# Output projection of a two-layer decoder step: weights in 4 + 4 row tiles, split while values are summed; the first quarter in two passes of tokens; GpSimd reads four page numbers ahead

## The chip, the cores and the metric

The kernel runs on one core of one Trainium2 chip. The metric is the device time of one execution in microseconds (us), as the median of several runs. Engines: TensorE (PE; its weight loads are listed apart as PEld), VectorE (DVE), ScalarE (ACT), GpSimd (POOL) and SyncE (SP), which issues DMAs. Each engine has its own instruction queue, and the queues meet only at semaphores.

## What is computed

One inference step of a trunk of two layers, for 256 prompt tokens and 8 x 8 = 64 sample tokens, 320 token columns in all, with 1024 features. Cut to the part around the change:

```python
for l in range(DEPTH):                      # 2 layers
    x = x + 0.5 * swiglu(rmsnorm(x), ...)   # ffn 1
    h = rmsnorm(x)
    # past: pages of keys and values of 8 sample sequences, 8 pages of 128 positions each
    oa = moba_attend(...)                   # heads 0..5
    of = fox_attend(...)                    # heads 6..10
    oc = hgrn2_recurrence(...)              # heads 11..15
    x = x + concat(oa, of, oc) @ w_out[l]   # (tokens x 1024) @ (1024 x 1024)
    x = x + 0.5 * swiglu(rmsnorm(x), ...)   # ffn 2
y = rmsnorm(x)
```

## The kernel before

Everything is written by hand in one block per engine, in program order, with counted semaphores. Features lie on the 128 partitions, tokens in the free dimension. A float32 product is made of three matmuls in a rounded type (`fp32r`): for each weight tile `whi` x `xh`, `wlo` x `xh` and `whi` x `xl`, where `hi` is the value rounded by an ACT copy, and `lo` is what DVE gets by subtracting `hi` from the value.

Weights go through two slots, 0 and 1. SP loads `raw[s]`, ACT rounds it to `whi[s]` (helper `hi`, line 609 before), DVE makes `wlo[s]` (helper `lo`, line 894), and PE multiplies (helper `dense`, line 1505). SP may load `raw[s]` again when `wlo[s]` is made (`split_done[s]`), and ACT may write `whi[s]` again when PE has used both (`w_free[s]`, which the order of instructions below prints as `weights_free`). The semaphore `raw_in[s]` tells that `raw[s]` has landed, `wout_in` that the extra pieces of the output weights have.

Attention over the past works in 32 blocks of two pages for each layer, four blocks a query (one query is one of the 8 sample sequences, `q`). PE turns the keys (line 1664) and makes scores (1688). For the query before, it turns the weights (`turn_weights`, 1699 and 1703), sums the values over 8 pages (`values`, 1715 and 1717, then the new ones, 1721 and 1723) and turns the outputs (`turn_outputs`, 1731). DVE copies weights (`copy_weights`, 1182 and 1185), scales the outputs (`scale_outputs`, 1194) and copies them (`copy_outputs`, 1203 to 1206). The prompt's attention and the recurrence are done among these blocks and are ready before the last query. Value pages are loaded by GpSimd (`load_values`, lines 582 and 583): for each page it waits until the query before has used that page (`values_used`), reads the page number from a table (`value_load`) and issues two DMAs. Value pages of query 7 are loaded after PE has used those of query 6, in two halves of four pages.

Behind query 7 comes the output projection, in four quarters `p` of 256 output features. A quarter has 8 tiles of 128 input rows: five in slot 0 and three in slot 1. The input is `mixed`, rounded to `oh` by ACT (prompt tokens at line 829, sample tokens at 869), and DVE makes `ol` (prompt 1408 in `prompt_out_lo`, sample 1471). Input tile 5 is made of rows 640 to 703 and 960 to 1023, and so has a DMA of its own for each half. Each quarter has two output tiles `j` in two PSUM banks; when one is complete (`acc_ready`, or `w_free[1]` for the second), DVE adds it to the residual `X` and makes the squares and the next `xl` (`accumulate`: lines 916, 908, 909, 903), and ACT makes the next `xh` (623). Over all 320 tokens a quarter is 8 x 2 x 3 = 48 matmuls. DVE's order in a quarter is `lo(1, u)`, `lo(0, u + 1)`, `accumulate`, where `u` is the quarter's use of the slots and `u + 1` the next one, so slot 0 is split a quarter ahead. After the last quarter come the gate weights of ffn 2, eight tiles in each slot.

## Time and profile before

| | |
|---|---|
| median of 3 runs | 1786.49 us (1783.93 to 1787.73) |
| profiled execution | 1789.04 us, of which its span, first to last instruction, is 1787.4 us |
| mean granted clock of TensorE over the span | 0.959 of full speed |
| busy: PE, DVE, ACT, POOL | 1663.8, 1084.8, 669.8, 162.1 us |
| instructions | 36002 |

All times in the rows below are from the start of the span of the profiled execution. A row of a timeline has an instruction's start, its duration, and in brackets how long its engine was idle before it and what ended that. Matmuls are pipelined, so the difference of two starts, not the duration, is what one costs in a stream. A granted clock of 1.00 is 2.4 GHz and one of 0.50 is 1.2 GHz.

### The profile page before, as it was taken

To read this page: it belongs to the slowest core of one execution; us is meant where nothing else is said; L and a number is where in the kernel's file an instruction comes from. 1 tells how busy PE (TensorE), PEld (TensorE's weight loads), DVE (VectorE), ACT (ScalarE), POOL (GpSimd) and SP (SyncE) were. 2 spreads that over 40 slices of the span, in tenths; PEclk is the share of its full clock that TensorE was granted. 3 is DMA by queue.
4 is the path that set the end of the run, shared out by engine and by line. 5 is a ranking of instruction groups with operands and counts; after the bars stand their busy time and mean duration, and the time that the engine had idled before them with its cause. 6 is when DMAs were issued, how large, how long until landed. Compare 5 with 4: busy or idle time off the path is not lost. (4 is left out here: it accounts for less than half of the span.)

```text
span 1787.4 us, 36002 instructions
## 1 busy us (share of the span) xinstructions
PE 1663.8 (93%) x13569; PEld 1537.6 (86%) x13569; DVE 1084.8 (61%) x1815; ACT 669.8 (37%) x960; POOL 162.1 (9%) x329
## 2 busy tenths in 40 slices
PE   5999999979989789999999999999798887999997
PEld 5999999966667579999999999999566666999996
DVE  7666555456577556665566665543676755766645
ACT  3333232235544424333333323322565443433332
POOL 0000000021333300000000000000224331000000
PEclk9999999989989889999999999999899997999998
DMA  6444445546666634444444444554657574444443
GB/s 191 141 154 152 139 145 141 156 135 185 216 195 214 195 125 160 146 143 151 140 154 155 150 135 153 159 141 126 188 182 243 191 217 147 160 159 141 138 151 116
DMA packets 284179, 287.46 MB, mean 161 GB/s; under 512 B 26542, under 2 KB 272998, under 8 KB 283942
## 3 DMA queue, kind: packets, MB, share of 16 engines
q1 hardware_dynamic: 268290, 239.52, 43.2%
q0 software_dynamic: 14464, 46.48, 8.2%
q8 instruction: 64, 1.05, 0.2%
q10 hardware_dynamic: 1316, 0.03, 0.1%
q14 instruction: 45, 0.37, 0.1%
HBM read 279.58 MB, written 6.40 MB: 160 GB/s over the span
## 5 line engine op out<-in xcount | busy, mean ns | idle before, releaser
L1505 PE MATMUL PS<-xh,whi 128*128 128x320 f32 x1920 | 596.4, 311 | 13.8 <-DMA K<-in_consts 10.2
L1505 PE MATMUL PS<-xh,wlo 128*128 128x320 f32 x1920 | 593.9, 309 | 0.0
L1505 PE MATMUL PS<-xl,whi 128*128 128x320 f32 x1920 | 593.8, 309 | 0.0
L609 ACT ACTIVATE whi<-raw 128x2048 fp32r<-128x2048 f32 (+2 forms) x185 | 340.5, 1841 | 610.0 <-PE PS L1505 602.9
L894 DVE TENSOR_TENSOR wlo<-raw,whi 128x2048 fp32r<-128x2048 f32 (+2 forms) x185 | 406.8, 2199 | 262.0 <-ACT whi L609 260.0
L1505 PEld LDWEIGHTS PS<-xh,whi 128*128 128x128 f32 x1920 | 361.0, 188 | 15.9 <-issue 10.4
L1505 PEld LDWEIGHTS PS<-xh,wlo 128*128 128x128 f32 x1920 | 361.1, 188 | 0.6
L1505 PEld LDWEIGHTS PS<-xl,whi 128*128 128x128 f32 x1920 | 361.0, 188 | 0.0
L1505 PE MATMUL PS<-hh,whi 128*128 128x320 f32 x704 | 217.5, 309 | 0.0
L1505 PE MATMUL PS<-hh,wlo 128*128 128x320 f32 x704 | 217.5, 309 | 0.0
L1505 PE MATMUL PS<-hl,whi 128*128 128x320 f32 x704 | 217.5, 309 | 0.0
L1664 PE MATMUL PS<-K,key_pages 128*128 128x128 f32 x768 | 114.8, 302 | 34.3 <-DVE P L1206 13.2
L1664 PEld LDWEIGHTS PS<-K,key_pages 128*128 128x128 f32 x768 | 94.2, 155 | 50.4 <-issue 41.8
L1505 PEld LDWEIGHTS PS<-hh,whi 128*128 128x128 f32 x704 | 132.2, 188 | 0.0
L1505 PEld LDWEIGHTS PS<-hh,wlo 128*128 128x128 f32 x704 | 132.2, 188 | 0.0
L1505 PEld LDWEIGHTS PS<-hl,whi 128*128 128x128 f32 x704 | 132.2, 188 | 0.0
L721 ACT ACTIVATE keys_t<-PS 128x512 f32<-128x512 f32 x128 | 75.3, 595 | 149.8 <-PE PS L1664 149.7
L575 POOL COPY key_pages<-past 128x10 f32<-128x10 f32 x64 | 17.0, 269 | 1181.3 <-DVEq L889 996.3
L931 DVE TENSOR_TENSOR tmp<-PS,rstd 128x320 f32<-128x320 f32 x88 | 42.6, 487 | 87.8 <-PE PS L1505 87.6
L627 ACT ACTIVATE tmp<-tmp 128x320 f32<-128x320 f32 x88 | 40.4, 463 | 116.3 <-DVE tmp L931 116.2
L582 POOL DMA_DIRECT2D value_pages<-in_cache_moba_v x128 | 70.1, 548 | 130.1 <-issue 71.9
L1052 DVE TENSOR_TENSOR P<-PS,rstd 128x320 f32 (+1 forms) x64 | 31.0, 488 | 79.2 <-PE PS L1505 77.9
(252 smaller groups left out, 1832.5 us busy)
## 6 DMA issues: line engine op xcount, KB each, us to landing
raw<-in_ffn_w_gate SPq DMA_DIRECT2D x45, 1024.0 KB
raw<-in_ffn_w_up SPq DMA_DIRECT2D x45, 1024.0 KB
raw<-in_ffn_w_down SPq DMA_DIRECT2D x32, 1024.0 KB
raw<-in_w_in SPq DMA_DIRECT2D x64, 512.0 KB
key_pages<-in_cache_moba_k SPq DMA_DIRECT2D x128, 192.0 KB, 2.5
value_pages<-in_cache_moba_v POOLq DMA_DIRECT2D x128, 192.0 KB, 2.9
key_pages<-in_cache_fox_k SPq DMA_DIRECT2D x128, 160.0 KB, 3.2
value_pages<-in_cache_fox_v POOLq DMA_DIRECT2D x128, 160.0 KB, 3.4
```

The source lines that it names most:

```text
L575: pool.tensor_copy(key_pages[:, pg:pg + 2, AW + BW:AW + BW + BH], past_of[:, L, q, 2 * n:2 * n + 2, :]).then_inc(past_in, 1)
L582: pool.dma_start(value_pages[:, pg, 0:AW], vmv[:, ds(page + L * NPOOL, 1), :].rearrange("p a c -> p (a c)")).then_inc(v_in[pg], 16)
L609: act.activation(whi[s][:, 0:nk, :], raw[s][:, 0:nk, :], ACT.Copy).then_inc(hi_done[s], 1)
L627: act.activation(tmp[j][:, :], tmp[j][:, :], ACT.Silu).then_inc(silu_done, 1)
L721: act.activation(keys_t[i % 2][:, 4 * u:4 * u + 4, :], PS[:, bank, :].rearrange("p (j c) -> p j c", j=4), ACT.Copy).then_inc(read_act[bank ...
L894: dve.tensor_tensor(wlo[s][:, 0:nk, :], raw[s][:, 0:nk, :], whi[s][:, 0:nk, :].bitcast(F32), ALU.subtract).then_inc(split_done[s], 1)
L931: dve.tensor_tensor(tmp[j][:, :], PS[:, j, 0:NT], rstd[:, :], ALU.mult).then_inc(gate_scaled, 1)
L1052: dve.tensor_tensor(P[:, ds(i * (4 * NT) + n * NT, NT)], PS[:, n, 0:NT], rstd[:, :], ALU.mult).then_inc(win_used, 1)
L1505: last = te.matmul(out, w[wslot][r, kt, cols], x[r, at, :], start=start and n == 0 and m == 0, stop=stop and n == len(ktiles) - 1 and m == 2)
L1664: last = te.transpose(PS[:, bank, 128 * j:128 * j + 128], key_pages[:, pg % 4, 128 * pr:128 * pr + 128], ident)
```

## The change

1. The output weights of a quarter are 4 tiles in slot 0 and 4 in slot 1. Input tile 4 has a DMA of its own into `raw[1]`, so two extra pieces count on `wout_in`.
2. For the first quarter ACT rounds both slots ahead of the sample `oh`, and DVE splits both ahead of `scale_outputs` of query 7. DVE's `prompt_out_lo` moves from before `copy_outputs(6)` to behind `copy_weights(7)`.
3. PE computes the first quarter in two passes: 48 matmuls with the 256 prompt tokens, which wait for the prompt's `ol` alone, then 48 with the 64 sample tokens. In both, `j` is the outer loop and the slot the inner one. The other quarters are as before, four tiles a slot, written out and no longer in a loop.
4. GpSimd reads four page numbers before the first wait of a half, and then only waits and issues.

```diff
@@ wout_chunks (SP)
-                fill(0, u, [(raw[0][:, 0:5, :], rows(0, 640).rearrange("l (k p) n -> p (l k) n", p=128))])
+                tiles = lambda r0, n: rows(r0, n).rearrange("l (k p) n -> p (l k) n", p=128)
+                fill(0, u, [(raw[0][:, 0:4, :], tiles(0, 512))])
                 sp.wait_ge(split_done[1], u + 1)
-                sp.dma_start(raw[1][0:64, 0, :], rows(640, 64).rearrange("l p n -> (l p) n")).then_inc(wout_in, 16)
-                fill(1, u, [(raw[1][64:128, 0, :], rows(960, 64).rearrange("l p n -> (l p) n")),
-                            (raw[1][:, 1:3, :], rows(704, 256).rearrange("l (k p) n -> p (l k) n", p=128))])
+                sp.dma_start(raw[1][:, 0:1, :], tiles(512, 128)).then_inc(wout_in, 16)
+                sp.dma_start(raw[1][0:64, 1, :], rows(640, 64).rearrange("l p n -> (l p) n")).then_inc(wout_in, 16)
+                fill(1, u, [(raw[1][64:128, 1, :], rows(960, 64).rearrange("l p n -> (l p) n")), (raw[1][:, 2:4, :], tiles(704, 256))])
@@ load_values (GpSimd)
-                    for pg in range(4 * half, 4 * half + 4):
+                    numbers = [pool.value_load(pages[0:1, q * NPG + pg:q * NPG + pg + 1], min_val=0, max_val=NPOOL - 1) for pg in range(4 * half, 4 * half + 4)]
+                    for pg, page in enumerate(numbers, 4 * half):
                         pool.wait_ge(values_used, (L * DB + q) * NPG + pg + 1)
-                        page = pool.value_load(pages[0:1, q * NPG + pg:q * NPG + pg + 1], min_val=0, max_val=NPOOL - 1)
@@ ACT, behind the blocks
-                hi(0, L * USES + OFF["wout"], 5)
+                hi(0, L * USES + OFF["wout"], 4)
+                act.wait_ge(wout_in, 32 * (L * 4 + 1))
+                hi(1, L * USES + OFF["wout"], 4)
                 act.wait_ge(outputs_copied, (L + 1) * DB)
                 act.activation(oh[:, :, SEQ:NT], mixed[:, :, SEQ:NT], ACT.Copy).then_inc(out_hi_ready, 1)
                 for p in range(4):
-                    act.wait_ge(wout_in, 16 * (L * 4 + p + 1))
-                    hi(1, u, 3)
-                    hi(0, u + 1, 5 if p < 3 else 8)
+                    if p:
+                        act.wait_ge(wout_in, 32 * (L * 4 + p + 1))
+                        hi(1, u, 4)
+                    hi(0, u + 1, 4 if p < 3 else 8)
@@ DVE, behind the blocks
-                prompt_out_lo()
                 copy_outputs(q - 1)
                 norms(q)
                 copy_weights(q)
+                prompt_out_lo()
+                lo(0, L * USES + OFF["wout"], 4)
+                lo(1, L * USES + OFF["wout"], 4)
                 scale_outputs(q)
                 copy_outputs(q)
-                lo(0, L * USES + OFF["wout"], 5)
@@ PE, behind the blocks
+                te.wait_ge(out_lo_ready, L * 2 + 1)
+                for s in range(2):
+                    chunk(s, L * USES + OFF["wout"])
+                settle(te)
+                for j in range(2):
+                    te.wait_ge(acc_used, L * 24 + 8 + j + 1)
+                    for s in range(2):
+                        project_out(0, j, s, slice(0, SEQ))
                 te.wait_ge(out_lo_ready, L * 2 + 2)
                 settle(te)
-                with te.Fori(0, 2) as m:
+                for j in range(2):
+                    for s in range(2):
+                        last = project_out(0, j, s, slice(SEQ, NT))
+                        if j == 1:
+                            last.then_inc(w_free[s], 1)
+                        elif s == 1:
+                            last.then_inc(acc_ready, 1)
+                for p in range(1, 4):
+                    for s in range(2):
+                        chunk(s, L * USES + OFF["wout"] + p)
```

What stands on DVE behind the blocks of layer 1, from the copies of query 6 to the splits of the first quarters (`P` in lines 1203 to 1206 is `mixed`, `idle` the rows of outputs). Before:

```order
L1408 TENSOR_TENSOR ol<-P,oh 128x8x256 [waits out_hi_ready]
...
L1182 COPY weight_cols<-PS 128x448 [waits value_sums_ready,weights_turned,vector_step]
L1185 COPY weight_cols<-PS 64x112 [waits weights_turned]
L1194 TENSOR_SCALAR idle<-PS,row_stats 112x256 [waits outputs_turned,value_sums_ready]
...
L894 TENSOR_TENSOR wlo<-raw,whi 128x1280 [waits read_dve0,vector_step,hi_done0]
L1471 TENSOR_TENSOR ol<-P,oh 128x8x64 [waits out_hi_ready]
L1472 MEMSET sqsum 128x320
L894 TENSOR_TENSOR wlo<-raw,whi 128x768 [waits vector_step,hi_done1]
L894 TENSOR_TENSOR wlo<-raw,whi 128x1280 [waits hi_done0]
L916 SCALAR_TENSOR_TENSOR X<-PS,X 128x320 [waits acc_ready]
```

And now:

```order
L1186 COPY weight_cols<-PS 128x448 [waits value_sums_ready,weights_turned,vector_step]
L1189 COPY weight_cols<-PS 64x112 [waits weights_turned]
L1412 TENSOR_TENSOR ol<-P,oh 128x8x256 [waits out_hi_ready]
L898 TENSOR_TENSOR wlo<-raw,whi 128x1024 [waits hi_done0]
L898 TENSOR_TENSOR wlo<-raw,whi 128x1024 [waits hi_done1]
L1198 TENSOR_SCALAR idle<-PS,row_stats 112x256 [waits outputs_turned,value_sums_ready]
...
L1476 TENSOR_TENSOR ol<-P,oh 128x8x64 [waits read_dve0,vector_step,out_hi_ready]
L1477 MEMSET sqsum 128x320
L898 TENSOR_TENSOR wlo<-raw,whi 128x1024 [waits vector_step,hi_done0]
L920 SCALAR_TENSOR_TENSOR X<-PS,X 128x320 [waits acc_ready]
```

The prompt's `ol` moved behind the two weight copies, both splits of the first quarter stand ahead of the scaling of the outputs, and nothing but the copies is left between that scaling and the sample `ol`. The split of slot 0 for the second quarter is still ahead of the first `accumulate`.

What stands on PE behind the outputs of query 7, layer 1. Before:

```order
L1731 MATMUL PS<-K,idle 128x112
L1927 UNCONDITIONAL_BRANCH [waits out_lo_ready]
L1927 ISA
L1937 ISA [waits split_done0]
L1505 MATMUL PS<-oh,whi 128x320 [waits acc_used]
L1505 MATMUL PS<-oh,wlo 128x320
L1505 MATMUL PS<-ol,whi 128x320
```

And now:

```order
L1737 MATMUL PS<-K,idle 128x112
L1511 MATMUL PS<-oh,whi 128x256 [waits split_done1,out_lo_ready,split_done0,acc_used]
L1511 MATMUL PS<-oh,wlo 128x256
L1511 MATMUL PS<-ol,whi 128x256
...
L1511 MATMUL PS<-oh,whi 128x64 [waits out_lo_ready]
L1511 MATMUL PS<-oh,wlo 128x64
L1511 MATMUL PS<-ol,whi 128x64
...
L1511 MATMUL PS<-oh,whi 128x320 [waits acc_used,split_done0]
```

The first quarter was 48 matmuls of 320 columns behind one wait; it is now 48 of 256, a wait, and 48 of 64, each with its own weight load.

What stands on GpSimd for a page before:

```order
L581 TENSOR_LOAD pages [waits values_used]
L581 ISA x2
L582 ISA
L582 DMA value_pages<-in_cache_moba_v 128x384
L583 ISA
L583 DMA value_pages<-in_cache_fox_v 128x320
```

And now, where four loads of numbers stand ahead of the first wait:

```order
L580 TENSOR_LOAD pages
L580 ISA x2
...
L583 ISA [waits values_used]
L583 DMA value_pages<-in_cache_moba_v 128x384
L584 ISA
L584 DMA value_pages<-in_cache_fox_v 128x320
```

The wait moved from the reading of the number to the DMA.

## Rows read from the trace of the kernel before

Layer 1 is the stretch of 600 to 675 us, layer 2 that of 1474 to 1540 us.

**Rows 1.** The page, busy time by engine: us (share of the span) xinstructions.

```profile
PE 1663.8 (93%) x13569; PEld 1537.6 (86%) x13569; DVE 1084.8 (61%) x1815; ACT 669.8 (37%) x960; POOL 162.1 (9%) x329
```

**Rows 2.** The view of the tile `ol`, who waited for it (us, times).

```profile
  PE PS L1505: 7.2, 2
```

**Rows 3.** Timeline of PE: start us, us, engine, line, op, out<-in, xcount [idle before <-releaser].

```profile
634.05 0.63 PE L1505 MATMUL PS<-oh,whi 128*128 128x320 f32 x1 [3.60 <-DVE ol L1471]
...
1483.95 1.78 PE L1699 MATMUL PS<-K,tokp 112*128 112x112 f32 x8 [3.32 <-ACT tokp L759]
...
1495.13 0.61 PE L1731 MATMUL PS<-K,idle 112*128 112x112 f32 x2 [0.69 <-DVE idle L1194]
...
1499.35 0.63 PE L1505 MATMUL PS<-oh,whi 128*128 128x320 f32 x1 [3.62 <-DVE ol L1471]
```

**Rows 4.** Timeline of DVE, layer 2, same columns.

```profile
1486.13 0.63 DVE L1182 COPY weight_cols<-PS 128x448 f32<-128x448 f32 x1
...
1496.77 1.49 DVE L894 TENSOR_TENSOR wlo<-raw,whi 128x1280 fp32r<-128x1280 f32 x1 [0.19 <-DVE P L1206]
...
1498.18 0.68 DVE L1471 TENSOR_TENSOR ol<-P,oh 128x512 fp32r<-128x512 f32 x1
```

**Rows 5.** Timeline of PE, value pages in layers 1 and 2; then one group of the whole trace.

```profile
623.20 0.65 PE L1715 MATMUL PS<-value_pages,weight_cols 128*32 128x128 f32 x8 [1.82 <-DMA value_pages<-in_cache_fox_v]
...
1489.68 0.67 PE L1715 MATMUL PS<-value_pages,weight_cols 128*32 128x128 f32 x7
...
1490.32 0.67 PE L1715 MATMUL PS<-value_pages,weight_cols 128*32 128x128 f32 x7
...
1492.79 0.65 PE L1715 MATMUL PS<-value_pages,weight_cols 128*32 128x128 f32 x8 [0.40 <-DMA value_pages<-in_cache_fox_v]
...
L1715 PE MATMUL PS<-value_pages,weight_cols 128*32 128x128 f32 x768 | 48.6, 292 | 7.2 <-DMA value_pages<-in_cache_fox_v 4.2 <-DVE weight_cols L1182 1.3 <-DVE weight_cols L1185 1.2
```

**Rows 6.** Timeline of GpSimd, layer 1.

```profile
609.33 0.56 POOL L582 DMA_DIRECT2D value_pages<-in_cache_moba_v  x1 [14.50 <-PE PS L1717]
...
612.35 0.55 POOL L583 DMA_DIRECT2D value_pages<-in_cache_fox_v  x1 [2.47 <-issue]
...
613.52 0.55 POOL L582 DMA_DIRECT2D value_pages<-in_cache_moba_v  x1 [0.62 <-issue]
```

**Rows 7.** Windows: us, busy time by engine (x), granted clock PEclk, DMA share, GB/s.

```profile
615.40:639.40 24.00, 14.87 (x157) 12.29 (x158) 7.01 (x19) 3.87 (x7) 6.43 (x12) 0.50 0.46 145
...
1487.10:1494.40 7.30, 6.53 (x126) 5.56 (x126) 0.00 (x0) 0.00 (x0) 2.19 (x4) 0.50 0.49 149
...
1499.30:1502.90 3.60, 3.55 (x13) 3.55 (x14) 0.96 (x1) 0.00 (x0) 0.00 (x0) 0.50 0.69 223
...
1503.00:1508.20 5.20, 5.20 (x36) 5.01 (x35) 1.16 (x1) 1.27 (x1) 0.00 (x0) 1.00 0.13 46
```

**Rows 8.** Timeline of PE weight loads: start of the program, and after a stall in layer 2.

```profile
10.37 0.93 PEld L1567 LDWEIGHTS PS<-K,P 64*128 64x128 f32 x8 [0.33 <-issue]
...
1508.65 0.19 PEld L1505 LDWEIGHTS PS<-oh,whi 128*128 128x128 f32 x1 [0.64 <-issue]
1508.76 0.19 PEld L1505 LDWEIGHTS PS<-oh,wlo 128*128 128x128 f32 x1
```

**Rows 9.** Timeline of PE, the second quarter in layer 2.

```profile
1508.66 0.41 PE L1505 MATMUL PS<-oh,whi 128*128 128x320 f32 x1 [0.39 <-DVE wlo L894]
...
1514.32 0.41 PE L1505 MATMUL PS<-oh,whi 128*128 128x320 f32 x1 [1.00 <-DVE wlo L894]
```

**Rows 10.** Timeline of ACT and DVE, splits and accumulate in layer 2.

```profile
1505.73 1.27 ACT L609 ACTIVATE whi<-raw 128x1280 fp32r<-128x1280 f32 x1 [7.67 <-PE PS L1505]
...
1508.56 0.49 DVE L916 SCALAR_TENSOR_TENSOR X<-PS,X 128x320 f32<-128x320 f32 x1
...
1513.30 0.96 DVE L894 TENSOR_TENSOR wlo<-raw,whi 128x768 fp32r<-128x768 f32 x1
...
1523.03 1.49 DVE L894 TENSOR_TENSOR wlo<-raw,whi 128x1280 fp32r<-128x1280 f32 x1 [1.19 <-ACT whi L609]
```

More of the change, by code:

```diff
@@ L1475, in _ @@
                     u = L * USES + OFF["wout"] + p
-                    lo(1, u, 3)
-                    lo(0, u + 1, 5 if p < 3 else 8)
+                    if p:
+                        lo(1, u, 4)
+                    lo(0, u + 1, 4 if p < 3 else 8)
                     accumulate(L * 3 + 2, p, 1.0, 1, u, (xh, xl))
@@ L1923, in _, with project_out @@
                 turn_outputs(DB - 1)
+                halves = [[(k, k, ALLR) for k in range(4)], [(k, 4 + k, ALLR) for k in range(4)]]
+                def project_out(p, j, s, tokens):
+                    x = oh[:, :, tokens], ol[:, :, tokens]
+                    return dense(PS[:, 4 + 2 * (p % 2) + j, tokens], s, slice(128 * j, 128 * j + 128), x, halves[s], s == 0, s == 1)
+                te.wait_ge(out_lo_ready, L * 2 + 1)
+                for s in range(2):
+                    chunk(s, L * USES + OFF["wout"])
@@ L1925, in _ @@
+                settle(te)
[3 more added lines that the diff above has]
+                        project_out(0, j, s, slice(0, SEQ))
                 te.wait_ge(out_lo_ready, L * 2 + 2)
                 settle(te)
-                with te.Fori(0, 2) as m:
-                    for dp in range(2):
-                        for s in range(2):
-                            chunk(s, L * USES + OFF["wout"] + m * 2 + dp)
-                            if s == 0:
-                                kts = [(k, k, ALLR) for k in range(5)]
-                            else:
-                                kts = [(0, 5, ALLR), (1, 6, ALLR), (2, 7, ALLR)]
-                            for j in range(2):
-                                if s == 0:
-                                    te.wait_ge(acc_used, L * 24 + 8 + m * 4 + 2 * dp + j + 1)
-                                last = dense(PS[:, 4 + 2 * dp + j, 0:NT], s, slice(128 * j, 128 * j + 128), (oh, ol), kts, s == 0, s == 1)
-                                if j == 1:
-                                    last.then_inc(w_free[s], 1)
-                                elif s == 1:
-                                    last.then_inc(acc_ready, 1)
@@ new lines, in _ @@
+                for j in range(2):
[8 more added lines that the diff above has]
+                        chunk(s, L * USES + OFF["wout"] + p)
+                        for j in range(2):
+                            if s == 0:
+                                te.wait_ge(acc_used, L * 24 + 8 + 2 * p + j + 1)
+                            last = project_out(p, j, s, slice(0, NT))
+                            if j == 1:
+                                last.then_inc(w_free[s], 1)
+                            elif s == 1:
+                                last.then_inc(acc_ready, 1)
```

## The prediction

> **What bounds the kernel now.** I read the page first: PE is busy for 93% of the span [rows 1], so a change counts only where it moves PE's work or fills one of its waits. I then asked who waits for each tile that the diff touches, and read the two places in the order of time, once per layer (layer 1 at 600 to 675 us, layer 2 at 1474 to 1540 us). Before the output projection PE waits 3.6 us twice, 7.2 us in all, for the `ol` of the sample tokens [rows 2]. In layer 2 the last transposes start at 1495.13 and the first projection matmul at 1499.35 [rows 3]. In that hole DVE copies the outputs, splits the five weight tiles (1.49 us) and only then makes the sample `ol` (0.68 us) [rows 4]. Ahead of it PE sums the values of query 7 and waits for pages, three times in layer 1 and twice in layer 2 [rows 5]. GpSimd issues a page as two DMAs of 0.55 us with about 0.04 us between them and then 0.62 us for the page number, 1.76 us a page [rows 6]. The granted clock is low there: 0.50 over 615.4 to 639.4 us, and 0.50 over 1487.1 to 1494.4 us although PE is busy for 6.53 of those 7.3 us; dense matmuls then run at 1.2 GHz until about 1503 and at 2.4 GHz after [rows 7].
>
> **The change, part by part.** The sum is made for the profiled execution (span 1787.4 us, time 1789.04 us), 2.55 us above the median of the runs, 1786.49. Times are starts in the profile; S is the first matmul of the second quarter (1508.66 in layer 2), T the first on its slot 1 (1514.32) [rows 9].
>
> *`prompt_out_lo` behind `copy_weights`.* DVE's 2.28 us `ol` no longer stands ahead of the weight copies of query 7. The transposes that these need end at 1485.73 (1483.95 + 1.78 [rows 3]) and the copy starts at 1486.13 [rows 4], so values start about 0.4 us earlier (0.3 in layer 1). The `ol` and two splits of 1.2 us then take 4.7 us of DVE while PE sums values for 7.3 us [rows 7]: nothing is added. If values took under 4.7 us, the rest would fall on `scale_outputs` and the path.
>
> *Page numbers ahead.* Eight numbers cost GpSimd the same 0.56 to 0.62 us each, but the first four are read while it waits for the pages of query 6 to be used, and the other four come in one piece of about 2.3 us between page 3 and page 4. So the last page is issued some 4 x 0.6 = 2.4 us earlier. In layer 2 pages 6 and 7 came late, page 7 starting at 1492.79 after a wait [rows 5]; page 5 starts at 1490.32 and page 7 at 1492.79, 2.47 us for two pages, and an unhindered page takes 0.64 us (1489.68 to 1490.32), so the waits cost 1.2 us, and all of it goes: with the 0.4 us, values end 1.6 us earlier. In layer 1 the first `fox` DMA was held for 2.5 us [rows 6]. I take it that this comes again at the same DMA, since nothing in the diff touches it; the chain behind it is then 2.4 us earlier. The next 1 MB of output weights waits for the splits of the first quarter; it is now asked for when the early splits end, about 622 us, beside pages 6 and 7. Between no loss and 1 us (half the rate for 350 KB) I take 0.4: values end 2.0 us earlier in layer 1. PE's waits for value pages are 4.2 us in the whole trace [rows 5], 3.5 of layer 1 and 0.7 of layer 2 in these two sums, so the other 14 queries give nothing. The splits of slot 1 are issued early as well.
>
> *The first quarter in two passes.* Before: 48 matmuls of 320 columns, at 0.267 us each at 1.2 GHz and 0.147 at 2.4 GHz (3.6 us / 13, 5.2 us / 36 [rows 7]). Now 48 of 256 columns start right behind the transposes, 3.6 us earlier relative to them, and 48 of 64 columns follow. By columns the 256 cost 0.213 and 0.117 us. How long is the clock low? Before, it rose 3.6 us (layer 2, [rows 7]) and 5.3 us (layer 1, 634.05 to 639.4 [rows 3, 7]) after the first dense matmul; now values run up to the dense part without the hole, so I take 3.9 us: 18 matmuls slow, 30 fast, 7.4 us (6.6 to 8.1 for 2.0 to 5.4 us of low clock).
> The 64-column matmuls are not in the trace in this type. Below, by columns: 64/320 of 0.147, 0.03 us. Above: the pace of 320 columns, 0.147. But each needs its own load of 128 columns of weights. After a stall two loads start 0.11 us apart (1508.65, 1508.76), and eight 64-column matmuls at the start with 128-column loads of their own take (0.93 - 0.22)/7 = 0.10 us each [rows 8]. I take 0.115: 5.5 us for 48, where they are 20% of the columns.
> The page "TensorE: Matmul & The Clock Gate" of the Trainium skill, section "LDWEIGHTS (loading the stationary operand)", puts a load at its columns over 1.2 GHz, 107 ns for 128, whatever follows; the 0.11 us agrees, and the sum by it is 5.1 us. It speaks against splitting a quarter, since every weight is loaded twice.
> So PE needs 12.9 us for a quarter that took 8.9 (1499.35 to 1508.27, which is 1508.66 less the 0.39 idle [rows 9]), and the hole of 3.6 us pays for most of it.
>
> *When the second quarter can start.* Slot 0 is released by matmul 36 of the second pass, 12 before its end; before, by matmul 30 of 48. Then ACT makes `whi` and DVE `wlo`. Five tiles cost ACT 1.27 us and DVE 1.49, three cost DVE 0.96 [rows 4, 10]; four are 1.05 (a little over 4/5 of 1.27) and 1.22. From the start of the second pass: 35 x 0.115, then 0.29 for the matmul to end and ACT to see it (0.2 + 0.09), 1.05, 0.04, 1.22, and 0.13 until PE starts, as between the rows now: 6.8 us to S. So PE waits about 1.3 us here instead of the 0.39 us of idle time shown now [rows 9].
> Behind that wait stands DVE's queue: `lo(0, u+1)` is ahead of `accumulate`. S to T is then accumulate, 4.7 us (1508.56 to the next split at 1513.30) [rows 10], and `lo(1)` of four tiles, 1.22, with 0.1 us of hand-over: 6.05 us, where it was 5.66. PE's own work for slot 0 is 3.5 us, so it waits there 2.3 us, more than the 1.00 now [rows 9].
> Layer 2: two cold transposes from 1495.13 and 0.15 us of waits, so the first dense matmul could have started at 1495.7, 3.65 us before it did [rows 3]; less 1.6 is 1494.1. S = 1494.1 + 7.4 + 6.8 = 1508.3, T = 1514.35: no gain (1514.32). Layer 1: 634.05 - 3.65 = 630.4; 630.4 - 2.0 + 14.2 = 642.6, T = 648.65 against 649.80: 1.15 us gained.
>
> *From T on.* The FFN start hangs on a chain: split of slot 0 for the last quarter, load of the gate weights, their split, `accumulate`. That split ended at T + 10.2 (1523.03 + 1.49) [rows 10]. With four tiles PE releases slot 0 at T + 7.35 (48 x 0.147 + 0.3), the split ends at T + 9.8 and 0.4 us is gained; of this 0.2 stays, since PE's longer slot 1 (24 matmuls, not 18) ends later. Sum: layer 1 -1.35, layer 2 -0.15, together -1.5 us: 1787.5 us against 1789.04, or 1785.0 against the median of 1786.49.
>
> **The rivals.**
> *GpSimd's hold does not recur, and the clock rises early.* The hold of 2.5 us is seen once in this layer and not at the same DMA of the other layer, so it may be of the moment. Without it pages are ready when PE wants them, and layer 1 gains 2.3 us more; low clock of 2 us instead of 3.9 gives 0.8 per layer. Between -3.8 and -5.4 us: 1782 us. 20%.
> *The second pass hides its loads.* At 0.03 us each, 36 matmuls release slot 0 3.1 us earlier in both layers: -7.7 us, 1779 us. Against it stand both rows 8. 5%. The same page, in "Back-to-back issue gap", has a table with about 60 cycles at 2.4 GHz for up to 64 columns; that is this case if the loads did not count.
> *Slower: the clock stays at 1.2 GHz.* Values keep PE busy and the granted clock does not rise [rows 7]; the second pass streams 64 columns in the time of 270, so it may not count as work either. If it is low over both passes and into the second quarter: first pass 10.2 us (+2.8), release 36 x 0.167 (+1.9), 24 matmuls of slot 0 6.4 us against DVE's 6.05 (+0.4): +5.1 per layer, +8.7 in all, 1795 us. It decides once the low clock lasts over some 7 us of the two passes in both layers. A fall only after the second pass costs little: 24 slow matmuls fit under DVE's 6.05 us. 13%.
> *The change hides nothing:* output weights delay the pages by a full us and values gain only in layer 2: -0.5 us, 1786. Inside the forecast's own range.
>
> **How the numbers follow.** Forecast 62% (own range 1782.8 to 1787.5), early pages and clock 20%, hidden loads 5%, slow clock 13%. For 8 in 10 the range reaches to 1781.3 below and 1789.0 above, where a clock low for a few us more lies. 0.2% of 1786.49 is 3.6 us, about what a measurement of this kernel can tell from no change. Faster takes nearly all of the two upper cases and 3% of the forecast: 0.27. Slower is most of the clock case: 0.12. Within: 0.61.
>
> **What would show it.** The wait for the sample `ol` gone on PE; 48 matmuls of 256 columns from 1494 and 48 of 64 at 0.11 to 0.12 us; value pages without waits in layer 2 and one in layer 1 after the hold; PE idle about 1.3 us before S and over 2 us before T; the granted clock low again between the second pass and T. I am wrong if the second pass paces at 0.03 or over 0.13 us, if S comes before 1507 or after 1510, or if T does not follow S by 6 us.

## The result, and the profile after

The changed kernel takes 1793.5 us (median of 7 runs, 1790.61 to 1805.41) where the kernel before takes 1784.77 us (7 runs): a ratio of 1.0056, 95% interval 1.0030 to 1.0081. A second set of runs gave 1.0050 (1.0033 to 1.0066). It is slower by 9 to 10 us, where 1.5 us less was predicted. A ratio given here is not that of two medians; the two differ by up to 0.0011.

The page of the profile after, its part 1: PE is busier, not less [rows 1 before].

```profile
span 1794.0 us, 36178 instructions
PE 1677.0 (93%) x13665; PEld 1553.1 (87%) x13665; DVE 1084.5 (60%) x1815; ACT 669.1 (37%) x960; POOL 161.0 (9%) x329
```

The wait for the sample `ol` before the projection [rows 2] is gone. PE's timeline of layer 1 shows the values, the last transposes, the first matmul of the first pass, then the second pass and S (639.69):

```profile
611.87 0.65 PE L1721 MATMUL PS<-value_pages,weight_cols 128*32 128x128 f32 x8 [0.91 <-DVE weight_cols L1189]
...
616.12 0.42 PE L1721 MATMUL PS<-value_pages,weight_cols 128*32 128x128 f32 x8 [1.46 <-DMA value_pages<-in_cache_fox_v]
...
617.04 0.42 PE L1721 MATMUL PS<-value_pages,weight_cols 128*32 128x128 f32 x8 [0.40 <-DMA value_pages<-in_cache_fox_v]
...
620.23 0.65 PE L1721 MATMUL PS<-value_pages,weight_cols 128*32 128x128 f32 x8 [2.65 <-DMA value_pages<-in_cache_fox_v]
...
622.29 0.65 PE L1721 MATMUL PS<-value_pages,weight_cols 128*32 128x128 f32 x8 [1.20 <-DMA value_pages<-in_cache_fox_v]
...
624.64 0.61 PE L1737 MATMUL PS<-K,idle 112*128 112x112 f32 x2 [0.69 <-DVE idle L1198]
624.92 0.56 PE L1511 MATMUL PS<-oh,whi 128*128 128x256 f32 x1
...
634.93 0.28 PE L1511 MATMUL PS<-oh,wlo 128*128 128x64 f32 x1
635.04 0.28 PE L1511 MATMUL PS<-ol,whi 128*128 128x64 f32 x1
...
635.54 0.40 PE L1511 MATMUL PS<-ol,whi 128*128 128x64 f32 x1
635.76 0.40 PE L1511 MATMUL PS<-oh,whi 128*128 128x64 f32 x1
...
639.69 0.64 PE L1511 MATMUL PS<-oh,whi 128*128 128x320 f32 x1
```

Four waits for pages add up to 5.7 us, where the stage before had 3.5 us in three (1.82 [rows 5], 0.78 and 0.89). In the second pass the pace changes: the starts are 0.11 us apart, then 0.21. Windows of time over the passes (in each row: busy time of the engines, then the granted clock, the DMA share and GB/s), layer 1 and then layer 2:

```profile
624.93:628.40 3.47, 3.47 (x18) 3.47 (x17) 1.73 (x6) 0.63 (x1) 0.00 (x0) 0.50 0.02 5
628.40:632.00 3.60, 3.60 (x33) 3.60 (x32) 0.00 (x0) 0.00 (x0) 0.00 (x0) 1.00 0.00 0
632.20:635.20 3.00, 3.00 (x30) 3.00 (x28) 0.00 (x0) 0.00 (x0) 0.00 (x0) 1.00 0.00 0
635.20:639.40 4.20, 4.20 (x23) 4.20 (x22) 0.99 (x1) 1.06 (x1) 0.00 (x0) 0.50 0.00 0
639.70:645.40 5.70, 5.70 (x22) 5.70 (x22) 4.83 (x9) 2.07 (x3) 0.00 (x0) 0.50 0.27 92
...
1500.90:1506.60 5.70, 5.70 (x50) 5.70 (x49) 1.73 (x6) 0.63 (x1) 0.00 (x0) 1.00 0.16 50
1506.63:1511.90 5.27, 5.27 (x50) 5.27 (x48) 0.00 (x0) 1.06 (x1) 0.00 (x0) 1.00 0.01 3
1513.20:1519.20 6.00, 6.00 (x22) 6.00 (x23) 5.08 (x9) 2.07 (x3) 0.00 (x0) 0.50 0.26 87
```

The clock rises in the first pass (layer 1) or is high throughout it (layer 2). It falls amid the 64-column matmuls, in which PE is never idle (layer 1, at 635.2), or behind them (layer 2, at 1512.4, where PE waits 1.13 us for S), and stays at 1.2 GHz over the first half of the second quarter in both layers. Before, it was high from S to T in both layers; layer 2:

```profile
1508.66:1514.32 5.66, 4.66 (x31) 4.40 (x31) 4.73 (x9) 2.77 (x4) 0.00 (x0) 1.00 0.37 116
```

**Where the time is.** I put a ruler on the output stage: every time below is a start on PE, counted from the start of the last weight transposes (615.33 and 1483.95 before [rows 3], 609.00 and 1490.83 after). "Last value" is the last matmul with a value page, "first dense" the first of the output projection, T the first on slot 1 of the second quarter; the sum adds the last mark, the first matmul of ffn 2, over both layers. Layer 1 / layer 2, us:

| kernel | last value | first dense | T | first FFN matmul | sum of the last | ratio to before (95%) |
|---|---|---|---|---|---|---|
| before | 12.7 / 9.4 | 18.7 / 15.4 | 34.5 / 30.4 | 54.2 / 50.2 | 104.5 | 1 |
| after | 13.9 / 8.4 | 15.9 / 10.1 | 36.9 / 28.7 | 58.5 / 50.2 | 108.7 | 1.0056 (1.0030 to 1.0081) |
| e5, after again | 14.7 / 7.9 | 16.8 / 9.5 | 37.7 / 28.7 | 58.9 / 50.1 | 109.0 | 1.0050 (1.0033 to 1.0066) |
| e1, numbers alone | 11.6 / 8.5 | 17.6 / 13.8 | 33.4 / 28.7 | 53.4 / 48.7 | 102.0 | 0.9995 (0.9980 to 1.0010) |
| e18, e1 again | 11.5 / 8.3 | 17.5 / 14.0 | 33.4 / 29.7 | 53.3 / 49.9 | 103.1 | 1.0013 (0.9998 to 1.0027) |
| e2, after, numbers one by one | 15.1 / 12.4 | 17.2 / 14.5 | 37.9 / 35.2 | 59.3 / 56.0 | 115.3 | 1.0059 (1.0036 to 1.0081) |
| e3, after, one pass | 14.3 / 9.2 | 19.3 / 14.1 | 33.6 / 28.8 | 54.5 / 51.2 | 105.7 | 1.0016 (0.9998 to 1.0033) |
| e4, wide second pass | 14.4 / 8.0 | 16.5 / 9.7 | 36.4 / 28.3 | 58.4 / 51.2 | 109.5 | 1.0046 (1.0028 to 1.0064) |
| e6, held load | 11.2 / 8.1 | 13.3 / 9.9 | 33.2 / 29.0 | 54.6 / 50.7 | 105.2 | 1.0020 (1.0000 to 1.0041) |
| e7, early 5 + 3 | 11.3 / 8.1 | 16.5 / 12.7 | 32.3 / 28.4 | 52.4 / 48.7 | 101.2 | 0.9991 (0.9972 to 1.0009) |
| e8, 4 + 4 alone | 12.7 / 9.8 | 18.5 / 15.6 | 32.6 / 29.7 | 53.9 / 50.8 | 104.7 | 1.0000 (0.9981 to 1.0019) |
| e9, held load, one pass | 11.7 / 8.6 | 16.7 / 13.0 | 31.3 / 26.7 | 53.5 / 47.5 | 101.0 | 0.9995 (0.9982 to 1.0009) |
| e10, both slots first | 11.2 / 8.9 | 16.2 / 13.3 | 28.8 / 26.6 | 51.1 / 48.7 | 99.9 | 0.9997 (0.9981 to 1.0012) |
| e11, slot order | 11.3 / 8.1 | 13.4 / 9.7 | 33.6 / 26.4 | 55.6 / 49.2 | 104.8 | 1.0012 (0.9995 to 1.0029) |
| e12, e9, last query ahead | 10.9 / 9.2 | 16.0 / 14.1 | 29.6 / 28.8 | 51.4 / 51.2 | 102.6 | 0.9997 (0.9981 to 1.0013) |
| e13, before, last query ahead | 11.3 / 8.5 | 17.3 / 13.9 | 33.1 / 29.3 | 53.4 / 49.8 | 103.2 | 0.9973 (0.9957 to 0.9989) |
| e17, e13 again | 11.5 / 8.2 | 17.0 / 13.7 | 32.6 / 29.2 | 53.5 / 49.3 | 102.9 | 1.0003 (0.9986 to 1.0020) |
| e14, all but last ahead | 12.7 / 9.1 | 18.7 / 14.4 | 33.6 / 29.3 | 53.7 / 49.3 | 103.0 | 1.0009 (0.9992 to 1.0026) |
| e15, after, last query ahead | 13.8 / 7.9 | 15.9 / 9.8 | 36.8 / 28.8 | 58.6 / 50.7 | 109.3 | 1.0037 (1.0016 to 1.0057) |
| e16, e7, last query ahead | 11.2 / 8.3 | 16.4 / 12.9 | 31.5 / 28.6 | 51.6 / 48.7 | 100.3 | 0.9976 (0.9961 to 0.9990) |

The experiments ran on chips where the kernel before took 1788.2 to 1789.7 us, so kernels are compared by ratio (0.0010 is 1.8 us). The ruler comes from one profiled execution of each. The stages of the changed kernel are 4.3 us longer in all: +4.3 in layer 1, nothing in layer 2. That is less than half of the loss; the rest is not in the two places that the prediction spoke of.

### The profile page after: what moved, and what is told of

The parts are those of the page before. It is cut to its first block and busy times, and to the rows that moved or that the text cites. A ratio compares the mean times of both kernels' runs of the same rounds, so it can differ in the third digit from the quotient of the medians.

```text
span 1794.0 us, 36178 instructions
## 1 busy us (share of the span) xinstructions
PE 1677.0 (93%) x13665; PEld 1553.1 (87%) x13665; DVE 1084.5 (60%) x1815; ACT 669.1 (37%) x960; POOL 161.0 (9%) x329
## 5 line engine op out<-in xcount | busy, mean ns | idle before, releaser
L1511 PE MATMUL PS<-xh,whi 128*128 128x320 f32 x1920 | 597.1, 311 | 13.8 <-DMA K<-in_consts 10.0
L610 ACT ACTIVATE whi<-raw 128x2048 fp32r<-128x2048 f32 (+1 forms) x185 | 340.3, 1841 | 614.8 <-PE PS L1511 606.5
L898 DVE TENSOR_TENSOR wlo<-raw,whi 128x2048 fp32r<-128x2048 f32 (+1 forms) x185 | 406.5, 2199 | 267.7 <-ACT whi L610 266.4
L1511 PEld LDWEIGHTS PS<-xh,whi 128*128 128x128 f32 x1920 | 361.1, 188 | 15.9 <-issue 10.2
L1670 PE MATMUL PS<-K,key_pages 128*128 128x128 f32 x768 | 115.2, 302 | 32.6 <-DVE P L1210 14.5
L1670 PEld LDWEIGHTS PS<-K,key_pages 128*128 128x128 f32 x768 | 94.0, 154 | 49.3 <-issue 40.9
```

The costliest lines, as they stand in the source:

```text
L610: act.activation(whi[s][:, 0:nk, :], raw[s][:, 0:nk, :], ACT.Copy).then_inc(hi_done[s], 1)
L898: dve.tensor_tensor(wlo[s][:, 0:nk, :], raw[s][:, 0:nk, :], whi[s][:, 0:nk, :].bitcast(F32), ALU.subtract).then_inc(split_done[s], 1)
L1511: last = te.matmul(out, w[wslot][r, kt, cols], x[r, at, :], start=start and n == 0 and m == 0, stop=stop and n == len(ktiles) - 1 and m == 2)
L1670: last = te.transpose(PS[:, bank, 128 * j:128 * j + 128], key_pages[:, pg % 4, 128 * pr:128 * pr + 128], ident)
```

## The experiments

**Which part: page numbers, or passes?** e1 puts into the kernel before nothing but the page numbers ahead, e2 takes them out of the changed kernel. e3 has one pass over 320 columns, e4 lets the second pass compute the last 256 tokens (192 of them twice).

```diff
--- e3, in the changed kernel
-                for j in range(2):
-                    te.wait_ge(acc_used, L * 24 + 8 + j + 1)
-                    for s in range(2):
-                        project_out(0, j, s, slice(0, SEQ))
...
-                for p in range(1, 4):
+                for p in range(4):
--- e4, in the changed kernel
-                        last = project_out(0, j, s, slice(SEQ, NT))
+                        last = project_out(0, j, s, slice(NT - SEQ, NT))
```

e1: 

> The kernel before with one part of the change, the four page numbers read ahead of the pages. Theory A (the loss is in the two passes: the granted clock falls in the 64-column matmuls and stays at 1.2 GHz through the second quarter, 2.3 us per layer from S to the FFN): this part is harmless; value waits of layer 2 go (-1.2 us), layer 1 between -2.3 and 0: 1782.5 to 1784.5 us, no slower than before. Theory B (in the profile of the changed kernel the output stages hold only 4.3 of the 8.7 us; the rest comes from GpSimd, whose four reads in one piece put page 4 behind by 2.3 us at every query): slower than before by 3 to 5 us, 1788 to 1790.

e2: 

> The changed kernel with the page numbers read one by one again. Theory A: within 2 us of the changed kernel, 1792 to 1795. Theory B: 3 to 5 us faster, 1788.5 to 1790.5.

e3: 

> The changed kernel with the first quarter again in one pass of 320 columns, which waits for both halves of ol; tiles stay 4 + 4 and the splits early. Theory A: the second quarter runs at 2.4 GHz; the hole ahead of the projection is back but without the 1.5 us split in it; S to the FFN 25.5 us again: 6 to 9 us faster than the changed kernel, 1784.5 to 1787.5, about as before. Rival (the 4 + 4 tiles and early loads of 1 MB beside the value pages cost the time, not the passes): at most 2 us faster than the changed kernel, 1791.5 or more.

e4: 

> The changed kernel, but its second pass computes the last 256 tokens instead of the last 64, so 192 columns are computed twice (the result is the same). Theory A: a matmul of 256 columns costs 0.118 us where one of 64 costs 0.112 at 2.4 GHz (and both 0.213 at 1.2), and with it the clock does not fall in the second pass nor in the second quarter: second pass 5.7 us, S to the FFN 25.5 instead of 27.8 us in both layers, 4 to 6 us faster than the changed kernel, 1787.5 to 1789.5, though PE does more work. Rival (the second pass costs because every weight is loaded twice, whatever the clock): 0 to 1 us slower than the changed kernel.

e1 measured 0.9995: not the 3 to 5 us loss of theory B, but not the gain of theory A either, though its output stages are 2.4 us shorter. Theory B wanted e2 faster than the changed kernel, and it is not: it loses 4.0 us to pages in layer 2 (last value 12.4, not 8.4). But its output stages are 6.6 us longer than those of the changed kernel and its time is not, so B is not done with; it comes back below. e3 took 1.0016, some 6 to 7 us under the changed kernel: the passes are a large part of the loss, and the rival falls.

e4 was made to judge theory A, and A falls with it. The clock now stays at 2.4 GHz until PE stalls; windows over the first pass, the second with the wait behind it, and slot 0 of the second quarter with its wait:

```profile
1504.70:1510.50 5.80, 5.80 (x50) 5.75 (x49) 1.73 (x6) 0.63 (x1) 0.00 (x0) 1.00 0.22 69
1510.50:1517.00 6.50, 5.83 (x50) 5.62 (x48) 0.90 (x1) 1.06 (x1) 0.00 (x0) 1.00 0.01 3
1517.40:1523.20 5.80, 3.77 (x24) 3.50 (x24) 4.93 (x9) 3.02 (x4) 0.00 (x0) 1.00 0.29 90
```

PE's timeline has S and T:

```profile
1517.38 0.41 PE L1511 MATMUL PS<-oh,whi 128*128 128x320 f32 x1 [1.06 <-DVE wlo L898]
1523.38 0.55 PE L1511 MATMUL PS<-oh,whi 128*128 128x320 f32 x1 [2.21 <-DVE wlo L898]
```

24 matmuls at the high clock are done early and PE waits 2.2 us: T is S + 6.0, against S + 6.35 with the low clock (1513.20 to 1519.55), where PE does not wait at T. The time, 1.0046, is 1 to 2 us better by the ratios, less than they can tell. So the low clock behind the passes is real and nearly free: DVE's queue (`accumulate`, then the split of slot 1) would hold T at S + 6.0 anyway. e4 is no clean price of the clock over the whole stage, though: its wait is followed by 3.4 us at 1.2 GHz behind T (1523.5 to 1526.9), and T to the FFN takes 22.0 / 22.9 us, not 21.6 / 21.5.

**What delays the pages, and what the tiles do.** e6 holds the load of the second quarter's weights until the last value page is used. e8 has 4 + 4 tiles and no other edit. e7 is 5 + 3 with early splits (ACT rounds slot 1 early too, not shown): `weight_cols` shares its place with the upper tiles of `wlo[0]`, so the fifth tile must wait for the values. e5 is the changed kernel once more.

```diff
--- e6, in the changed kernel
                 for m in range(4):
+                    if m == 1:
+                        sp.wait_ge(values_used, (L + 1) * DB * NPG + NPG)
                     wout_chunks(L, m)
--- e7, in the kernel before, DVE (with the page numbers ahead)
-                prompt_out_lo()
                 copy_outputs(q - 1)
                 norms(q)
                 copy_weights(q)
+                prompt_out_lo()
+                dve.wait_ge(hi_done[0], L * USES + OFF["wout"] + 1)
+                dve.tensor_tensor(wlo[0][:, 0:4, :], raw[0][:, 0:4, :], whi[0][:, 0:4, :].bitcast(F32), ALU.subtract)
+                lo(1, L * USES + OFF["wout"], 3)
                 scale_outputs(q)
                 copy_outputs(q)
-                lo(0, L * USES + OFF["wout"], 5)
+                dve.tensor_tensor(wlo[0][:, 4:5, :], raw[0][:, 4:5, :], whi[0][:, 4:5, :].bitcast(F32), ALU.subtract).then_inc(split_done[0], 1)
```

e5: 

> The changed kernel once more, so that it stands beside the others against the same runs of the kernel before. 7 to 11 us slower than before. In its profile again: 64-column matmuls at 0.112 us (2.4 GHz) and 0.213 (1.2 GHz), S to T 6.2 us, T to the FFN 21.5 us (before 19.8).

e6: 

> The changed kernel, with SyncE holding the load of the second quarter's weights until all value pages are used. Theory C (the early splits let 1 MB of weights in beside the last value pages, and these land 2 to 3 us later): values of layer 1 end 11 to 12 us after the last transposes instead of 13.85, no wait for page 4 to 7 over 0.7 us apart from GpSimd's own, and 2 to 5 us are gained on the changed kernel. Rival (the pages are late because GpSimd issues them late, whatever the weights do): values end at 13 to 14 as now, and nothing is gained.

e7: 

> The kernel before with three things: page numbers ahead; the ol of the prompt behind the weight copies; and of the first quarter's 5 + 3 tiles the first four of slot 0 and all three of slot 1 split while values are summed (the fifth, whose place in wlo overlaps weight_cols, after them). One pass, 5 + 3 tiles in every quarter. Theory D (4 + 4 tiles bring the two last loads together, so that the gate weights land 2.3 us later; 5 + 3 does not): T to the FFN is 19.8 us as before, the first matmul of the projection comes 1.1 us earlier relative to the last value, and the time is 2 to 5 us under the kernel before. Rival (early splits cost in the value pages what they give): as before, within 2 us, or slower.

e8: 

> The kernel before with 4 + 4 tiles in place of 5 + 3 and nothing else. Theory D: T to the FFN 21.5 us instead of 19.8 in each layer, the split of the gate weights starting 7 us or more after the last split of slot 0 instead of 5.3: 3 to 4.5 us slower than before. Rival (the tail of the changed kernel comes from its late start or its clock, not from the tiles): within 1 us of before.

e6 gave what theory C said, and a little more than its 2 to 5 us: 1.0020, 5 to 6 us under the changed kernel; the values of layer 1 end at 11.2, not 13.9 or 14.7. The DMA view of the pages' last 14 us shows it, changed kernel (611 to 625 us, 1.05 MB of weights on the other queue) and e6 (617 to 631 us, its weights behind the pages); the number at the end is the median from issue to landing:

```profile
value_pages<-in_cache_moba_v POOLq DMA_DIRECT2D x4, 192.0 KB, 3.3
value_pages<-in_cache_fox_v POOLq DMA_DIRECT2D x4, 160.0 KB, 4.2
```
```profile
value_pages<-in_cache_moba_v POOLq DMA_DIRECT2D x4, 192.0 KB, 3.1
value_pages<-in_cache_fox_v POOLq DMA_DIRECT2D x4, 160.0 KB, 3.4
```

The rival of e6 (GpSimd issues the pages late) can be looked at in the same traces. The last `fox` DMA of the changed kernel and of e6, and PE's start on that page in e6:

```profile
616.27 0.55 POOL L584 DMA_DIRECT2D value_pages<-in_cache_fox_v  x1
```
```profile
621.99 0.55 POOL L586 DMA_DIRECT2D value_pages<-in_cache_fox_v  x1
...
625.41 0.65 PE L1723 MATMUL PS<-value_pages,weight_cols 128*32 128x128 f32 x8 [0.23 <-DMA value_pages<-in_cache_fox_v]
```

Both are issued 7.3 us after the last transposes (609.00 and 614.71). PE starts on the page 6.0 us after the issue in the changed kernel (622.29, above) and 3.4 us after it in e6. So the pages are not issued later, they land later.

PE's waits for them, changed kernel and e6:

```profile
L1721 PE MATMUL PS<-value_pages,weight_cols 128*32 128x128 f32 x96 | 7.4, 330 | 6.6 <-DMA value_pages<-in_cache_fox_v 5.7 <-DVE weight_cols L1189 0.9
```
```profile
L1723 PE MATMUL PS<-value_pages,weight_cols 128*32 128x128 f32 x96 | 7.4, 330 | 4.0 <-DMA value_pages<-in_cache_fox_v 3.1 <-DVE weight_cols L1191 0.9
```

e8 confirms half of theory D. From T to the FFN it takes 21.2 / 21.1 us instead of 19.8 / 19.9, but its T comes 1.8 and 0.7 us earlier, and the time is that of before (1.0000, not 1.002). 4 + 4 tiles alone cost nothing that shows within the interval of 0.0019. e7 has no such tail by design, but its time, 0.9991, cannot be told from before.

**Passes with the pages undisturbed.** e9 is e6 with one pass, e10 moves both slots' splits for the next quarter ahead of `accumulate`, e11 is e6 with the second pass slot by slot.

```diff
--- e10, in e9, DVE (and ACT alike)
                 for p in range(4):
-                    if p:
-                        lo(1, u, 4)
                     lo(0, u + 1, 4 if p < 3 else 8)
+                    if p < 3:
+                        lo(1, u + 1, 4)
                     accumulate(L * 3 + 2, p, 1.0, 1, u, (xh, xl))
--- e11, in e6, second pass
-                for j in range(2):
-                    for s in range(2):
+                for s in range(2):
+                    for j in range(2):
                         last = project_out(0, j, s, slice(SEQ, NT))
```

e9: 

> The changed kernel with the load of the second quarter's weights held until all value pages are used, and the first quarter in one pass. Theory E (the second pass adds as much of PE as the hole that the first one fills, and the low clock then makes it more): the first matmul comes 3 to 4 us later than with two passes, T comes 1 to 3 us earlier in layer 1 and within 1 us in layer 2, 2 to 5 us are gained on the changed kernel with the held load (ratio to before 1.002), so 1 to 3 us under the kernel before. Rival (with the load held, two passes are as good as one or better): ratio to before 1.002 or above.

e10: 

> The kernel with the held load and one pass, and on ACT and DVE both slots' splits for the next quarter ahead of accumulate, where now slot 1's stands behind it. If S to T is set by DVE's queue (accumulate, 4.7 us, ahead of the split of slot 1), the waits of 1.1 to 1.75 us on the first matmul of slot 1 go in all three quarters: T to the FFN 19 us or less instead of 21, 4 to 6 us under the same kernel without this. If the loads of the output and gate weights set it, the waits move to slot 0 and to the FFN, and at most 1 us is gained.

e11: 

> The changed kernel with the held load, and the second pass going slot by slot, so that slot 0 is free after 24 of its 48 matmuls and not after 36. If my sum was right that S hangs on that release, the wait of 1.4 us ahead of S in the layers where the pass runs at 2.4 GHz goes, and S follows the last 64-column matmul at once: 1 to 2.5 us faster than with the held load alone (1.002 to before), 1.0006 to 1.0014. Rival (PE's own work bounds S): no change in S where the pass runs at 1.2 GHz, and under 0.7 us in all.

e9 is the fair comparison of one pass and two: 0.9995 against 1.0020, 4.5 us with intervals that just overlap, and 4.2 us in the ruler. With the held load and one pass the whole loss is gone (1.0050 to 1.0056 in the changed kernel), so these two carry most of it. Its first matmul is 3.4 and 3.1 us later, its T 1.9 and 2.3 us earlier. In layer 2 its whole quarter of 48 matmuls of 320 columns takes 8.5 us:

```profile
1494.83:1503.30 8.47, 8.47 (x48) 8.47 (x49) 2.04 (x4) 1.36 (x2) 0.00 (x0) 0.81 0.07 20
```

e10: the wait at T goes (from 31.3 to 28.8 in layer 1) and comes back 5 us later as a gap of 1.8 us between two starts ahead of the third quarter, in both layers; the sum gains 1.1 us and the time nothing. The rival was right: loads and splits, not the order in the queue, pace the quarters. e11 starts S 2.5 us earlier in layer 2 (20.5, not 23.0) and 1.1 us later in layer 1, where more of its passes ran at 1.2 GHz; 1.0012 against 1.0020 settles nothing.

**Reading ahead where nobody waits.** All kernels that read ahead for every query took longer than their output stages say. e12 to e15 read ahead for the last query only, or for all but the last:

```diff
+                    read = lambda pg: pool.value_load(pages[0:1, q * NPG + pg:q * NPG + pg + 1], min_val=0, max_val=NPOOL - 1)
+                    ahead = q == DB - 1
+                    numbers = [read(pg) if ahead else None for pg in range(4 * half, 4 * half + 4)]
                     for pg, page in enumerate(numbers, 4 * half):
                         pool.wait_ge(values_used, (L * DB + q) * NPG + pg + 1)
+                        if page is None:
+                            page = read(pg)
```

e12 (in e9): 

> The kernel with the held load, 4 + 4 tiles and one pass (0.9995 of before), and the page numbers read ahead for the last query of a layer only, one by one for the seven before it. Theory F (reading ahead costs 2 to 3 us in the block stages, which single profiles hide since these vary by 8 us): output stages 3.5 us shorter than before as now, and the time follows: 0.9975 to 0.9985 of before, the best so far. Rival (reading ahead costs nothing there): 0.9990 to 1.0000, as now.

e13 (in the kernel before): 

> The kernel before with the page numbers read ahead for the last query of a layer alone. Theory F: the 2.4 us that the output stages were shorter with all of them ahead, and nothing lost: 0.9980 to 0.9992 of before. Rival: as with all queries, 0.9990 to 1.0000.

e14 (in the kernel before, `q < DB - 1`): 

> The kernel before with the page numbers read ahead for all queries but the last of a layer. Theory F: 1.0010 to 1.0025 of before (2 to 4 us slower), though no value page is waited for in these queries. Rival: 0.9993 to 1.0007.

e15 (in the changed kernel): 

> The changed kernel with reading ahead for the last query alone. Theory F: 1.0030 to 1.0042 of before, where the changed kernel has 1.0050 to 1.0056. Rival: 1.0045 to 1.0060.

e16 (in e7): 

> The kernel with 5 + 3 tiles, seven of the eight split early, one pass (0.9991 of before), and page numbers read ahead for the last query alone. Theory F: its output stages were 3.3 us shorter than before, and nothing is lost elsewhere: 0.9970 to 0.9985. Rival: 0.9988 to 1.0000, as with all of them ahead.

e17 (e13 again): 

> The kernel before with page numbers read ahead for the last query alone, once more. If 0.9973 was its true place: 0.9965 to 0.9982. If it was a chance reading of a kernel that gains the 1.5 to 2.4 us of its output stages: 0.9982 to 0.9995.

e18 (e1 again): 

> The kernel before with page numbers read ahead for all queries, once more and on the same chip as the one for the last query alone. Theory F: 0.9990 to 1.0003, and at least 0.0010 above the other. Rival (reading ahead costs nothing in the block stages): the two within 0.0008 of each other.

e15 and e16 fell into theory F's ranges, e14 missed its by 0.0001 and e13 went past its, but e12 did not move (0.9997), and e17 put the very kernel of e13 at 1.0003. e17 and e18 both lie above the ranges given for them (up to 0.9995 and 1.0003), though 0.0010 apart as theory F said. The interval of one ratio reaches 0.0014 to 0.0023 either way, and the same kernel came out 0.0030 apart in e13 and e17, so single pairs don't decide: all queries ahead against the last alone gives e1 and e13 +0.0022, e18 and e17 +0.0010, e5 and e15 +0.0013, e7 and e16 +0.0015, e9 and e12 -0.0002. Over all runs it is clearer. I take each ratio times 1787 us less 1787 and subtract the change of its ruler's sum from 104.5. The 12 sets of runs with reading ahead for all queries, or for all but the last, have 1.5 to 5.8 us left, 3.0 in the mean. The 7 with it for the last alone or not at all have -3.5 to 2.1 us left, 0.2 in the mean. So reading ahead for the other queries seems to cost about 3 us outside the output stages. This is a pattern over 19 sets of runs of 16 kernels, and the profiled executions do not confirm it. Their span less the sum of the ruler is 1685.4 us in the mean of the 12 and 1684.2 in that of the 7 and the kernel before, 1.2 us apart with a spread of 2 to 3 us within each group; their block stages of both layers together are 400.4 and 399.7 us. Where the 3 us would fall, and why, stays open.

## Why the prediction was wrong

Its layer 2 came out (predicted 0.15 us earlier at the FFN, measured 0.04), by terms that cancel; its layer 1 and the time outside did not. Step by step:

- *Values start 0.4 us earlier behind `prompt_out_lo`; ol and splits hidden under the values*: right. Values start 2.88 us after the transposes in both layers, before 3.27 and 3.19.
- *"Between no loss and 1 us (half the rate for 350 KB) I take 0.4": this is the step that failed first.* The early splits free both slots, and the 1 MB of the second quarter's weights leaves when GpSimd issues the last four pages. I had named the collision with pages 6 and 7, and priced it at half the rate for 350 KB, which is one page (192 + 160 KB). Values of layer 1 were to end 2.0 us earlier and ended 1.1 us later (2.0 in e5), 3.1 us wrong. With the load held (e6) they end 1.5 us earlier, so the collision cost 2.6 us (3.5 in e5) and not 0.4. GpSimd's hold came again, as taken: 2.48 us idle ahead of the first `fox` DMA of query 7. In layer 2 values end 0.9 us earlier (1.5 in e5), for 1.6.
- *Two passes*: first pass 7.30 / 5.73 us for 7.4. 64 columns at 0.112 us, for 0.115, but only at 2.4 GHz; at 1.2 GHz each takes 0.213, as one of 256 columns does. I had no price for that, and put 0.167 for it in the clock rival. From the second pass to S 7.47 / 6.57 us, for 6.8; from the first matmul to S 14.8 / 12.3 for 14.2, so layer 2 gained 1.9 us that was not forecast. S to T 6.2 / 6.35 for 6.05.
- *"Of this 0.2 stays", from T on: this failed too, in both layers.* T to the first FFN matmul is 21.6 / 21.5 us where 19.6 was predicted and 19.8 was before. The split of slot 0 for the last quarter ended at T + 9.6, as predicted (9.8). What I left out is the load behind it. DVE now makes this split right behind that of slot 1, so SyncE issues slot 1's four DMAs first and the gate weights only after them; SyncE's timeline, and ACT's row that waits for the gate weights:

```profile
1528.04 0.34 SPq L454 DMA_DIRECT2D raw<-in_w_out  x1
1528.42 0.47 SPq L455 DMA_DIRECT2D raw<-in_w_out  x1
1528.93 1.23 SPq L430 DMA_DIRECT2D raw<-in_w_out  x2
1530.52 0.42 SPq L430 DMA_DIRECT2D raw<-in_ffn_w_gate  x1
...
1536.72 1.91 ACT L610 ACTIVATE whi<-raw 128x2048 fp32r<-128x2048 f32 x1 [2.50 <-DMA raw<-in_ffn_w_gate]
```

  The split ended at 1529.16, the gate load is issued 1.36 us later and is split 6.2 us after that. In the kernel before, the split ended at 1524.52 [rows 10], the load was issued 0.2 us later (1524.70) and split 5.2 us after that (1529.89), 5.4 us in all; here it is 7.6. e8 has the same tail and wins it back ahead of T, which the changed kernel cannot, since its T hangs on a late S.
- *"So the other 14 queries give nothing"*: by the pattern above they take about 3 us, which is not shown in a trace. I had costed the reads as the same work in another order.
- *The sum.* Layer 1: 2.9 (first matmul) + 0.6 (passes) + 0.2 (S to T) + 2.0 (tail) = 5.7 us over the prediction, -1.35 became +4.3. Layer 2: -0.1 - 1.9 + 0.3 + 1.8 = +0.1. With about 3 us elsewhere that is 7.3 us of the 9 to 10 measured. The rest is within what one profiled execution can tell: it reached the last transposes of layer 1 6.3 us earlier than the one of before, and the way from the FFN of layer 1 to the last transposes of layer 2 8.9 us longer.

By the prediction's own signs S was too early in layer 2: it came 22.4 us after the transposes, and 1507 us is 23.05. Its remark that a fall of the clock behind the second pass costs little, since the slow matmuls fit under DVE's 6.05 us, was right (e4).

The clock rival named 1795 us, and the clock was low over the whole of slot 0 of the second quarter as it said. But it asked for a low clock over both passes too, some 7 us in both layers: layer 1 had that (3.5 us of the first pass, 4.5 of the second), layer 2 had it in neither pass. So its price of 5.1 us a layer was never put to the test, and the low clock cost 0.9 us in the second pass of layer 1 (7.47 us to S against 6.57) and 0.2 to 0.35 us from S to T. That its 1795 us lie near the 1793.5 is chance.

Of the page "TensorE: Matmul & The Clock Gate" of the Trainium skill, section "LDWEIGHTS (loading the stationary operand)", the 107 ns for a load of 128 columns fits the 0.112 us here at a granted 2.4 GHz and not the 0.213 at 1.2 GHz: the pace of a load with its 64-column matmul goes with the granted clock. Worked out from its figure, an estimate, 48 more loads are 5.1 us of PE, which spoke against the change. The runs agree that the second pass costs more than the hole gives back: two passes took 4.5 us more than one (e6 against e9).

## A version that measured faster

e16 (page numbers ahead for the last query alone, the prompt's `ol` behind the weight copies, 5 + 3 tiles with seven of eight split early, one pass) took 1782.55 us where the kernel before took 1788.6: 0.9976, interval 0.9961 to 0.9990. Its output stages are 4.2 us shorter and its gain is 4.3. DVE's timeline shows the early splits, tile five aside, within 5 us of the weight copies:

```profile
614.29 2.27 DVE L1415 TENSOR_TENSOR ol<-P,oh 128x2048 fp32r<-128x2048 f32 x1
616.49 1.21 DVE L1474 TENSOR_TENSOR wlo<-raw,whi 128x1024 fp32r<-128x1024 f32 x1
617.62 0.94 DVE L901 TENSOR_TENSOR wlo<-raw,whi 128x768 fp32r<-128x768 f32 x1
```

It keeps slot 0 until the values are done, and so keeps the large load away from the pages. It is the best but one of 19 ratios (e13 had 0.9973), and e13 and e17 differ by 0.3% as one and the same kernel, so e16 has to be repeated before its gain is relied on.

## What to carry to other kernels

Ask of every buffer that a change frees earlier which load it lets go, and what that load meets; where it meets the pages that the critical engine waits for, hold it. Work that fills a hole must be smaller than the hole: 48 more matmuls to fill 3.6 us were not. And follow a chain past the last instruction that the change touches, to the load and the split behind it; the tail from T on was lost there.

## What the runs showed of the hardware

- In a stream, a matmul of 64 columns with its own load of 128 columns takes 0.112 us at a granted 2.4 GHz and 0.213 at 1.2; one of 256 columns 0.118 and 0.213 (changed kernel).
- PE can be busy without pause and still lose its clock: it fell to 0.50 at 635.2 us, in the 64-column matmuls, and did not fall there when the same pass streamed 256 columns (e4, layer 2, granted 1.00 over 1510.5 to 1517.0).
- A load of 1 MB on SyncE's queue beside the pages on GpSimd's made PE start on the last page 6.0 us after its issue, and 3.4 us without that load (changed kernel, e6).
- The block stages, the same in all kernels but for the reads of page numbers, took 195.6 to 203.3 us in layer 1 and 196.7 to 205.4 in layer 2 over the 20 profiled executions, first to last transpose of key pages, and on the whole the longer ones have more time at a granted 1.2 GHz. From 395 to 600 us, e5 (195.6) and e1 (200.1):

```profile
395.00:600.00 205.00, 181.47 (x2305) 131.88 (x2307) 137.36 (x373) 104.71 (x275) 61.96 (x127) 0.95 0.67 206
```
```profile
395.00:600.00 205.00, 186.99 (x2247) 137.03 (x2245) 133.76 (x363) 99.69 (x265) 60.51 (x127) 0.89 0.66 206
```

  Single runs of the kernel before took 1781.8 to 1798.6 us, so one span proves nothing about an edit worth 3 us. Stretches counted from a mark of their own repeat better (the ruler's sum moved by 0.3 to 1.1 us in the three kernels that were profiled twice).
